# Every fourth expert row's v half summed by VectorE, and gate rows built in PSUM where they are used

## What is computed

```python
for l in range(DEPTH):
    mod = c_act @ ada_w[l] + ada_b[l]
    sh_m, sc_m, g_m, sh_f, sc_f, g_f = jnp.split(mod, 6, axis=-1)
    h = _rmsnorm(x, norm_mix_g[l]) * (1.0 + sc_m[:, None]) + sh_m[:, None]
    cols = h @ w_in[l]                      # 1024 x 3332
    ...                                     # differential attention | RWKV-7 | forgetting attention
    mix = jnp.concatenate([y_a, y_b, y_c], axis=-1) @ w_out[l]
    x = x + g_m[:, None] * mix
    h = _rmsnorm(x, norm_ffn_g[l]) * (1.0 + sc_f[:, None]) + sh_f[:, None]
    x = x + g_f[:, None] * peer_ffn(h, peer_wq[l], peer_subkeys[l], peer_u[l], peer_v[l])
```

```python
u = jnp.take(u_tab, eidx, axis=0)
act = jnp.einsum('thkd,td->thk', u, hc)
coef = gate * jax.nn.gelu(act, approximate=False)
vsel = jnp.take(v_tab, eidx, axis=0)
return jnp.einsum('thk,thkd->td', coef, vsel)
```

## Time and profile before

| | |
|---|---|
| median of 3 runs | 2044.91 us (2039.49 to 2047.84) |
| the profiled execution | 2040.21 us |
| its span, first to last instruction | 2038.4 us |
| TensorE busy | 1646.9 us (81%) |
| VectorE busy | 1426.0 us (70%) |
| ScalarE busy | 655.4 us (32%) |
| DMA queues, share of 16 engines' span | gathers and modulation weights 73.2%, sync engine's queue 16.7% |
| granted TensorE clock, mean | 0.922 |

### The profile page before, as it was taken

How to read it: one execution, slowest core, us unless ns; L and a number is a source line. 1 busy time by engine, 2 the same in 40 slices (tenths; PEclk the granted TensorE clock), 3 DMA queues, 4 the chain that set the end, 5 groups by cost and what they waited for, 6 DMA issues and landing times.

```text
span 2038.4 us, 20976 instructions
## 1 busy us (share of the span) xinstructions
PE 1646.9 (81%) x6868; PEld 1031.3 (51%) x6868; DVE 1426.0 (70%) x3407; ACT 655.4 (32%) x1591; POOL 526.1 (26%) x564
## 2 busy tenths in 40 slices
PE   1667676877998898778998898798899898778776
PEld 1556674544555564454555564554565563333332
DVE  5648588745998656673998745676997566777754
ACT  1222123332643323431553323432643323222222
POOL 2010013222232323122232222222222223333341
PEclk9787698988999999898899999899998999998899
DMA  9973689987799999896899999899789999999996
GB/s 376 352 267 118 229 308 368 366 337 265 274 351 387 402 338 412 341 377 231 307 341 386 408 349 405 346 378 335 268 332 363 401 383 398 422 422 421 422 421 250
DMA packets 181981, 706.08 MB, mean 346 GB/s; under 512 B 10992, under 2 KB 101616, under 8 KB 115696
## 3 DMA queue, kind: packets, MB, share of 16 engines
q0 software_dynamic: 86784, 587.24, 73.2%
q1 hardware_dynamic: 95088, 117.50, 16.7%
HBM read 703.64 MB, written 1.05 MB: 346 GB/s over the span
## 4 chain that ended last, share of the span: by engine, by line
PE 33%; DMA 31%; DVE 27%; issue 5%; ACT 3%; POOL 0%; SPq 0%; DVEq 0%; ACTq 0%; POOLq 0%
PE psum L764 16%; DMA W<-in_w_in_dram 13%; DMA ringmem<-in_peer_uv_dram,eidx 9%; DVE ringmem L1422 7%; DMA W<-in_peer_wq_dram 6%; PE psum L405 5%; PE psum L640 4%; PE psum L627 2%; DMA ringmem<-in_ada_wt_dram 2%; DMA W<-in_w_out_dram 2%; PE psum L408 1%; DVE ringmem L1056 1%; DVE W L1186 1%; ACT diag L1027 1%; DVE attn L1196 1%
## 5 line engine op out<-in xcount | busy, mean ns | idle before, releaser
L764 PE MATMUL psum<-ringmem,diag 128*128 128x512 f32 x2048 | 975.2, 623 | 124.3 <-ACT diag L1027 124.2
L372 POOL DMA_INDIRECT ringmem<-in_peer_uv_dram,eidx x512 | 491.5, 960 | 1233.1 <-PE psum L764 1191.0
L764 PEld LDWEIGHTS psum<-ringmem,diag 128*128 128x128 f32 x2048 | 392.4, 200 | 594.3 <-issue 416.3
L1422 DVE SCALAR_TENSOR_TENSOR ringmem<-ringmem,psum 128x1024 f32<-128x1024 f32 x512 | 610.0, 1220 | 110.9 <-DMA ringmem<-in_peer_uv_dram,eidx 90.4
L405 PE MATMUL psum<-hT,W 128*128 128x128 f32 x1344 | 180.3, 295 | 99.1 <-DMA W<-in_w_in_dram 75.1
L1027 ACT ACTIVATE diag<-K,coef 128x128 f32<-128x128 f32 x512 | 176.1, 392 | 247.2 <-DVE coef L1435 247.1
L405 PEld LDWEIGHTS psum<-hT,W 128*128 128x128 f32 x1344 | 175.7, 210 | 125.7 <-DMA W<-in_w_in_dram 82.0
L1435 DVE SCALAR_TENSOR_TENSOR coef<-coef,ginv,gexp 128x2 f32<-128x2 f32 x256 | 56.7, 221 | 187.5 <-ACT coef L1019 181.5
L1019 ACT ACTIVATE coef<-dots 128x2 f32<-128x2 f32 x256 | 51.6, 202 | 333.5 <-DVE ringmem L1422 329.4
L640 PE MATMUL psum<-hT,W 128*128 128x128 f32 x1024 | 132.5, 289 | 26.1 <-DMA W<-in_peer_wq_dram 24.5
L640 PEld LDWEIGHTS psum<-hT,W 128*128 128x128 f32 x1024 | 129.0, 205 | 36.3 <-DMA W<-in_peer_wq_dram 20.7
(11 more groups left out here) (245 smaller groups left out, 1662.5 us busy)
## 6 DMA issues: line engine op xcount, KB each, us to landing
ringmem<-in_ada_wt_dram POOLq DMA_DIRECT2D x48, 1024.0 KB
W<-in_w_in_dram SPq DMA_DIRECT2D x24, 1536.0 KB
W<-in_peer_wq_dram SPq DMA_DIRECT2D x32, 1024.0 KB
W<-in_w_out_dram SPq DMA_DIRECT2D x16, 1024.0 KB
W<-in_w_in_dram SPq DMA_DIRECT2D x12, 1024.0 KB
ringmem<-in_peer_uv_dram,eidx POOLq DMA_INDIRECT x512
W<-in_w_in_dram SPq DMA_DIRECT2D x4, 1040.0 KB
attn<-in_subkeys_t_dram SPq DMA_DIRECT2D x4, 1024.0 KB
```

The costliest lines, as they stand in the source:

```text
L372: nc.gpsimd.indirect_dma_start(slot(k), None, rows, bass.IndirectOffsetOnAxis(ap=eidx[:, ph % 2, m:m + 1], axis=0)).then_inc(row_landed[q ...
L764: mm = nc.tensor.matmul(acc[:, q], diag[:, k % DIAGS, :], slot(k)[:, D:][:, q], start=(k % SEL == 0), stop=(k % SEL == SEL - 1), skip_grou ...
L1422: ins = v.scalar_tensor_tensor(out=u, in0=u, scalar=1.0, in1=hrep, op0=ALU.mult, op1=ALU.mult, accum_out=dots[:, j:j + 1])
```

## The change

Three things:

1. Of every four rows, the last (`k % 4 == 3`, the second row of every odd tick) is no longer weighed by TensorE. VectorE does it right behind the tick's coefficients: `accv = v_half * coef + accv` over 128x1024 in SBUF (`weigh` on VectorE), the first of a phase without the addition, and frees the slot. ScalarE makes no diagonal matrix for it.
2. `add_sum` gets a third operation: `accv = acc + accv`, then times the gate, then plus the residual.
3. `grow` and its copies are gone. All eight blocks of a gate are made in `tm` (free from segment 50 on), TensorE multiplies all eight at once into two banks (4 and 5 for `g_m`, 6 and 7 for `g_f`), and VectorE reads them there. For `g_m` the blocks move from segments 46 and 47 to 50 and 51 and the product to 52; for `g_f` the product moves to 77. `add_mix` first copies the gate's half from PSUM to `hm`, since the other factor is in PSUM too.

```diff
+        accv = sb("accv", [P, D])
-        gdiag = (hT[:, 0:4, :], hm[:, 0:512].rearrange("p (a c) -> p a c", a=4))
+        gdiag = tm[:].rearrange("p g k c -> p (g k) c")[:, 0:KD, :]
+        def on_vector(k):
+            return k % 4 == 3
...
                         elif seg == 46:
                             state_next(0)
-                            gate_row(g_at(i, 0), gdiag[0], bank[4], ("u_sb", at("u_sb", i, 1)))
                         elif seg == 47:
                             state_sum(1)
-                            gate_row(g_at(i, 1), gdiag[0], bank[4], ("g_sb", g_at(i, 1)))
...
                             out_product(seg - 51)
+                            if seg == 52:
+                                gate_row(g_at(i, 0), 4)
...
                     for k in range(n * BATCH, (n + 1) * BATCH):
+                        if on_vector(k):
+                            continue
                         for b in range(2):
                             q = slice(b * 512, (b + 1) * 512)
                             mm = nc.tensor.matmul(acc[:, q], diag[:, k % DIAGS, :], slot(k)[:, D:][:, q],
...
+                        elif seg == 50:
+                            if i == 0:
+                                act.wait_ge(s["mod_ready"], 2)
+                            act.wait_ge(s["y_out"], at("y_out", i, 1))
+                            act.wait_ge(s["st_out"], st_at(i, 2 - t))
+                            gate_diag(l, G_M, 0)
...
                         dve.wait_ge(s["wo_out"], at("wo_out", i, 2 * half + 2))
-                        dve.wait_ge(s["g_sb"], g_at(i, half + 1))
-                        step(v.tensor_tensor(hm[:, q], bank[6 + half][:, :], grow[:, q], ALU.mult), "wo_taken")
+                        dve.wait_ge(s["g_out"], g_at(i, 1))
+                        step(v.tensor_copy(hm[:, q], bank[4 + half][:, :]))
+                        step(v.tensor_tensor(hm[:, q], bank[6 + half][:, :], hm[:, q], ALU.mult), "wo_taken")
...
+                def weigh(k):
+
+                    j = k % (NBUF * BATCH)
+                    c = coef[:, j:j + 1]
+                    if k % SEL == 3:
+                        ins = v.tensor_scalar(accv[:], slot(k)[:, D:], c, None, ALU.mult)
+                    else:
+                        ins = v.scalar_tensor_tensor(out=accv[:], in0=slot(k)[:, D:], scalar=c, in1=accv[:],
+                                                     op0=ALU.mult, op1=ALU.add)
+                    ins.then_inc(freed(k)[0], 1)
+                    dve.wait_ge(*freed(k))
+
                 def add_sum(ph):
                     t = ph % NT
-                    dve.wait_ge(*freed((ph + 1) * SEL - 1))
-                    dve.wait_ge(s["g_sb"], g_at(ph + 1, 4) if ph + 1 < PHASES else g_at(PHASES, 2))
-                    step(v.tensor_tensor(hm[:], acc, grow[:], ALU.mult), "sums_taken")
-                    step(v.tensor_tensor(xs[:, t, :], xs[:, t, :], hm[:], ALU.add), "x_done")
+                    dve.wait_ge(*freed((ph + 1) * SEL - 2))
+                    step(v.tensor_tensor(accv[:], acc, accv[:], ALU.add), "sums_taken")
+                    dve.wait_ge(s["g_out"], g_at(ph + 1, 2) if ph + 1 < PHASES else g_at(PHASES, 1))
+                    step(v.tensor_tensor(accv[:], psum[:, 6 * 512:8 * 512], accv[:], ALU.mult))
+                    step(v.tensor_tensor(xs[:, t, :], xs[:, t, :], accv[:], ALU.add), "x_done")
```

81 lines of the change are left out of this document (35 added, 46 removed).

## The result

| | before | after |
|---|---|---|
| median of the runs made side by side | 2046.38 us (4 runs, 2039.49 to 2057.32) | 2085.47 us (4 runs, 2078.42 to 2091.4) |
| ratio to before, 95% interval | | 1.0185 [1.0123, 1.0247] |
| the profiled execution | 2040.21 us | 2078.42 us |
| its span | 2038.4 us | 2076.6 us |

The change makes the kernel 1.85% slower. The direction was forecast; the size was not: 39 us between the medians, 38.2 us between the two spans, where 11.4 us were worked out. 2085 us lies above the range's end of 2079 us.

The account below looks back on a forecast made before the run. VectorE was taken to bound the attention part, full DMA engines the output projection, queries and last phase; the projection loses DMA gaps. 35.4 - 5.4 - 12 - 7 + 3 - 2.6 = +11.4 us, so 2056 us against the median; range 2030 to 2079.

Parts of the forecast that it names:

- VectorE's new instruction: Attention parts: nine weighings of 1.31 us a phase lie on VectorE's full stretch, +35.4 us for three phases.
- The one of tick 39 falls into a wait of 3.64 us: End of attention part: this weighing hides in VectorE's wait for TensorE and costs nothing; without that cover, 1.3 us a phase.
- Gate rows out of the levels: Levels: without the gate products there, tick 38's weighing could start about 1.1 us sooner; together -5.4 us, bounds 0 and -8.
- TensorE's relief in the gaps: Projection: TensorE's spared rows of 1.72 us shorten DMA gaps by about 4 us a phase, -12 us for three.
- In the queries: Queries: a spared weighing at tick 51 and weights asked for sooner give 2.3 us a phase, -7 us for three.
- Moved gate rows: Output projection: gate product 2.3 us and copies 0.7; free where DMA engines are full, about +3 us in the first mixing.
- The end: After the last coefficients: TensorE ends 3.9 us sooner with two rows on VectorE; with add_sum's third operation, -2.6 us.
- Weighings fit behind the gathers: Last phase: twenty weighings, 26.2 us, fit into VectorE's 36.4 us of waits for gathers in 200 us; cost 0.
- Earlier weights: Rival: weights requested sooner close half the gaps, 39 us, with VectorE's price at its lower bound; 2026 us, chance 0.15.
- Nothing moves: Rival: TensorE's relief of 1.72 us and VectorE's load of 1.31 per odd tick cancel; 2045 us, chance 0.06.
- The last phase turns to VectorE: Rival: weighings over 1.8 us make VectorE bound the last phase; at 2.0 us each, 2081 us, chance 0.04.
- VectorE takes it all back: Rival: VectorE's chain in projection and queries keeps gaps from shrinking, and the gates give nothing; 2080 us, chance 0.2.

Follow-up runs that it names:

- f5_warm_uw: The changed kernel with four unused TensorE products of constants ahead of the products of segment 44; 2087.97 us, ratio to before 1.0185.
- e1_gates: The changed kernel with TensorE weighing all rows again, so only the moved gate rows and add_sum's third operation (as a copy) remain; 2059.81 us, ratio to before 1.0041.
- f7_inside: The changed kernel with VectorE weighing only in odd ticks 21 to 39 of the first three phases; 2083.46 us, ratio to before 1.0110.
- e2_load: The changed kernel with TensorE weighing all rows and VectorE running the same instruction on a constant, result unused; 2103.32 us, ratio to before 1.0245.
- e3_relief: The changed kernel with VectorE multiplying one column in place of each weighing, leaving every fourth row's v half out; 2052.7 us, ratio to before 1.0017.
- e4_outside: The changed kernel with TensorE alone weighing in ticks 21 to 39 of the first three phases; 2046.19 us, ratio to before 0.9965.
- f6: The changed kernel with two groups of four unused TensorE products where the old gate products stood, first mixing only; 2082.34 us, ratio to before 1.0142.
- f8: The changed kernel with TensorE alone weighing in ticks 21 to 39 of three phases, plus unused products in the first mixing; 2041.74 us, ratio to before 0.9983.

## Why the prediction was wrong

**VectorE's new instruction: right in price and place.** 1287 ns measured, 1284 taken. The first seven odd ticks of the stretch cost 8.9, 7.9 and 8.3 us in the three phases (ticks 22 to 35), where 7 x 1.31 is 9.2. The dummy load in place of the weighing gives the same length, the restriction to other ticks takes it away. The mark set in the prediction was +10 us in each attention part; it came out at +14. The other mark there, VectorE's waits still under 4 us, wasn't kept: they are 5.7 us (2.9, 2.5 and 0.3), where they were 3.0.

**"The one of tick 39 falls into a wait of 3.64 us", and no other wait was expected to grow: the step that failed.** This is where the largest miss is. I gave ticks 36 to 39 one weighing of 1.31 us a phase and credited the gates' -5.4 us in all, together -1.5 us. They got 17.0 us longer, and ticks 40 to 47 give only 3 us of it back. The wait of 3.64 us shrank to 2.7, so it covers 1 us a phase of the weighing of tick 39, and not 1.31. Of the 17.0 us, 7.9 are the two weighings a phase; the other 9.1 us are the chain that alternates between the engines, and f5_warm_uw takes 5.9 of them away again. TensorE's products there wait for a VectorE step that is now late, find TensorE's clock fallen after a longer standstill, and VectorE waits for them: 2.9 us instead of 0.4. I had priced what VectorE takes, and not what the engines that it releases do when it is late. My bound for a phase was 13.1 us; 14 were measured.

**"Gate rows out of the levels", -5.4 us: wrong, it is 0 to -1.7.** VectorE sets the pace there, and TensorE's steps were covered. In e1_gates the two waits of VectorE for TensorE in ticks 36 to 39 are what they were, and the next one is 4.8 us in place of 3.64. I had inferred from a later row (TensorE could weigh 1.1 us sooner) a gain for the phase, without asking whether anybody waits for that weighing; my own reading of the earlier trace rows said nobody does.

**"TensorE's relief in the gaps", -12 us in the projection: about right, and hidden by scatter.** Seven kernels with VectorE weighing in those ticks under its full load have 514.7 to 523.4 us there, mean 518.6; before, e1_gates and f7_inside, without, have 521.9 to 535.1, mean 529.7 (e2_load and e3_relief, with one half of the edit each, are left out). That is -11 us on the mean, from one profile of each kernel. The profile of before stood at the low end of its group, so that against it only -6 showed.

**In the queries, -7 us: wrong, 0.** Kernels with the relief there and an attention part as before have 491.7 to 492.9, before and e1_gates 490.2 and 491.9. The spared time is spent in waiting for the query weights (24.5 to 50.6 us). I had read "DMA share 1.00" as full engines and still credited 2.3 us a phase for a gap; in the second phase the share is now 0.95 and the part no shorter.

**"Moved gate rows", +3 us in the first mixing: the term was mis-sized, it is +6.6.** The sum of product and copy was right (2.3 + 0.7 taken, 1.95 + 0.69 measured), but I had credited -0.6 for the levels, and they lost 4.5 us (15.01 in place of 10.51), because the products that I counted as a cost had kept TensorE at its upper clock level: unneeded products in their place bring it back to 10.04. Part of that doesn't show in +6.6, since this execution of the changed kernel reached the levels 2.1 us sooner. Over all kernels, the seven with moved gate rows and nothing in their place have 328.6 us on the mean, the three with the old ones 321.8.

**The end: right. The beginning of the last phase: missed.** From the last coefficients to `add_sum` it is 2.8 us, where it was 6.4:

```profile
2062.65 0.22 DVE L1435 SCALAR_TENSOR_TENSOR coef<-coef,ginv,gexp 128x2 f32<-128x2 f32 x1 [0.27 <-ACT coef L1016]
...
2063.36 1.98 PE L769 MATMUL psum<-ringmem,diag 128*128 128x512 f32 x4 [0.94 <-ACT diag L1026]
2065.45 1.23 DVE L1454 TENSOR_TENSOR accv<-psum,accv 128x1024 f32<-128x1024 f32 x1 [1.26 <-PE psum L769]
```

-3.6 us, and -2.3 with the third operation; -3.9 and -2.6 were forecast. But the first two ticks of the last phase, in which `add_sum` of the phase before stands, take 12.9 us instead of 10.0 (the third operation, a gather that comes 0.7 us late, and the first weighing of 0.75 us), and ticks 2 to 47 take 231.8 instead of 229.2. Weighings fit behind the gathers, as said: VectorE's wait for them in the middle of the last phase, 36.4 us in the earlier trace rows, is down by about the 26 us that were put in.

```profile
DVE ringmem L1422 <- DMA ringmem<-in_peer_uv_dram,eidx: 10.8, 17, 1.1
```

**The rivals.** "Earlier weights" wanted half of the gaps, 39 us; the two parts together gave 11. "Nothing moves" failed for the reason given against it. "The last phase turns to VectorE" had its condition (1.8 us a weighing) unmet. "VectorE takes it all back" named 2080 us, five under the result, for a cause that held in the queries and for the gates and not in the projection. The mark of failure that I had set (projection shorter by over 8 us) can't be judged from one profile of each: the three projections are 11 and 6 us shorter and 11 us longer. The range failed because every bound was set by TensorE's and VectorE's durations, and none allowed for a chain's waits to grow.

Put together by stretch, the missing 26.8 us are: attention with the gates' term 12.1, projection against this profile of before 5.9, last phase 4.3, first mixing 3.6, queries 0.9.

**What stays open.** The four kernels none, outside, inside and both (e1_gates, e4_outside, f7_inside, after) have ratios 1.0041, 0.9965, 1.0110 and 1.0185. If the two halves of the change added up, both together would be 1.0034; it is 1.5% more, with an uncertainty of about 1.1% from the four intervals (by the medians it would be 0.9%). The profiles put that into the queries (476 us with the inside half alone, 484 to 493 with both) without saying why.

## What to carry to other kernels

A transfer of work to an engine with 70% average load costs its full duration in every stretch in which that engine sets the pace; put it into the other stretches alone, and the same edit gains (1.0185 against 0.9965, and 0.9919 with the gates left alone). In a chain that goes to and fro between engines, count what is late on both sides: a standstill of the partner can cost it its clock. And before a short product is counted as a saving, look at what it keeps awake behind it.

## What the runs showed of the hardware

- The first weighing of a phase, which has one tensor operand where the others have two, takes 0.75 us over the same 1024 columns where the others take 1.28. The page "VectorE: DVE Perf Modes" of the Trainium skill, by which the prediction had said that only this one would be short (section "Mode 2×_2P — use both read ports for one tensor"), agrees.

```profile
1752.41 0.75 DVE L1444 TENSOR_SCALAR accv<-ringmem,coef 128x1024 f32<-128x1024 f32 x1
```

- Unneeded products shortened a stretch: with two groups of four products of constants in the first mixing, it took 10.04 and 10.22 us (f6, f8) from one step of VectorE to another, where it took 15.01 us in seven kernels without them.
- Either more work on VectorE or less on TensorE lengthened TensorE's standstill ahead of the same twelve products: 0.95 us before, 3.14 with the load alone, 3.81 with the relief alone, 4.89 with both. VectorE's wait for them went from 0.4 us to 2.9, 2.0 and 2.9.
- The mean granted clock is a poor measure of time: 0.866 in a kernel at 1.0017 (e3_relief), 0.878 in the fastest one (0.9919), 0.922 in the kernel before.
